# A two-block transformer kernel: where the inverse-root multiplication runs, and five orders on VectorE and ScalarE

## The reference

```python
def rmsnorm(x, g):
    y = xf * lax.rsqrt(jnp.mean(xf * xf, axis=-1, keepdims=True) + EPS)
    return (y * g)

def swiglu(x, w_gate, w_up, w_down):            # D_FF = 2816
    return (jax.nn.silu(x @ w_gate) * (x @ w_up)) @ w_down

# first block
x = x + 0.5 * swiglu(rmsnorm(x, ff1_norm), ff1_w_gate, ff1_w_up, ff1_w_down)
h = rmsnorm(x, mix_norm); a_in, q, k, v, g_logits = split(h @ w_in)
y_a = gmlp_spatial_gating(gelu(a_in), ln_g, ln_b, w_s, b_s)   # layernorm(v) inside
y_b = stick_breaking_attention(q, k, v)
merged = g_a * (y_a @ w_branch_a) + g_b * (y_b @ w_branch_b)
x = x + merged @ w_out
x = x + 0.5 * swiglu(rmsnorm(x, ff2_norm), ff2_w_gate, ff2_w_up, ff2_w_down)
x = rmsnorm(x, final_norm)
# second block: h + attention @ w_o, h + squared_relu_mlp, twice, and a last rms_norm
```

## Time and profile before

| what | us |
|---|---|
| median of 3 runs (1243.75 to 1244.47) | 1244.16 |
| the profiled execution | 1244.19 |
| its span | 1242.4 |
| TensorE busy in the span | 1224.5 (99%) |
| VectorE busy | 816.7 (66%) |
| ScalarE busy | 625.8 (50%) |
| GpSimd busy | 171.1 (14%) |

### The profile page before, as it was taken

One profiled execution on the slowest core, in us unless ns is written; L12 is line 12 of the kernel. 1 busy time (PEld: TensorE's weight loads), 2 busy tenths in 40 slices (PEclk: granted clock), 3 DMA queues, 4 the chain that ended last, 5 costly groups with the idle time before them and its releaser, 6 DMA issues.

```text
span 1242.4 us, 17592 instructions
## 1 busy us (share of the span) xinstructions
PE 1224.5 (99%) x6847; PEld 1047.5 (84%) x6847; DVE 816.7 (66%) x1229; ACT 625.8 (50%) x965; POOL 171.1 (14%) x224
## 2 busy tenths in 40 slices
PE   8999999999999999999999999999999999999997
PEld 7888888888878888888878988888888888888886
DVE  6766666344676667766676766875765576876764
ACT  6544436554644347444446566544446365744443
POOL 1222210122030003222102310000000541000000
PEclk9999999999999999999999999999999999999999
DMA  7755566533847455655665435865562555675540
GB/s 248 246 180 184 189 201 186 185 105 94 295 132 224 146 170 174 201 192 188 195 195 153 137 119 186 268 189 189 186 200 76 171 164 163 195 252 189 191 147 35
DMA packets 174907, 221.74 MB, mean 178 GB/s; under 512 B 9084, under 2 KB 103896, under 8 KB 174824
## 3 DMA queue, kind: packets, MB, share of 16 engines
q1 hardware_dynamic: 173496, 216.86, 55.2%
q0 software_dynamic: 880, 2.70, 0.8%
q10 hardware_dynamic: 448, 1.05, 0.2%
HBM read 219.52 MB, written 1.06 MB: 178 GB/s over the span
## 4 chain that ended last, share of the span: by engine, by line
PE 88%; DVE 6%; ACT 4%; issue 1%; DMA 0%; POOL 0%; ACTq 0%; DVEq 0%; POOLq 0%
PE bank L1431 48%; PE bank L1517 22%; PE bank L1524 11%; DVE w_lo L961 3%; PE bank L1454 1%; PE bank L1688 1%; ACT w_hi L618 1%; PE bank L1671 1%; PE bank L1661 1%; DVE xt L996 1%; ACT xt L656 1%; DVE x L1073 1%; DVE a_uv L1317 1%; PE bank L1648 1%; PE bank L1646 1%
## 5 line engine op out<-in xcount | busy, mean ns | idle before, releaser
L961 DVE TENSOR_TENSOR w_lo<-raw,w_hi 128x1024 fp32r<-128x1024 f32 (+1 forms) x448 | 499.2, 1137 | 234.3 <-ACT w_hi L618 234.0
L618 ACT ACTIVATE w_hi<-raw 128x1024 fp32r<-128x1024 f32 (+1 forms) x448 | 420.5, 972 | 278.3 <-PE bank L1524 146.6
L1517 PE MATMUL bank<-xt,w_hi 128*128 128x512 f32 x1216 | 316.6, 392 | 0.4 <-ACT w_hi L618 0.4
L1517 PEld LDWEIGHTS bank<-xt,w_hi 128*128 128x128 f32 x1216 | 215.8, 189 | 35.1 <-ACT w_hi L618 0.6
L1524 PEld LDWEIGHTS bank<-xt,w_lo 128*128 128x128 f32 x1216 | 170.6, 190 | 15.3
L1524 PE MATMUL bank<-xt,w_lo 128*128 128x256 f32 x1216 | 175.1, 282 | 0.0
L1431 PE MATMUL bank<-w_hi,xt 128*128 128x512 f32 x512 | 160.1, 394 | 1.9 <-DVE w_lo L961 1.1
L1431 PE MATMUL bank<-w_hi,yt_lo 128*128 128x512 f32 x336 | 132.2, 394 | 0.0
L1431 PE MATMUL bank<-w_hi,yt_hi 128*128 128x512 f32 x336 | 130.9, 390 | 0.0
L1431 PE MATMUL bank<-w_lo,yt_hi 128*128 128x512 f32 x336 | 130.9, 390 | 0.0
L1431 PE MATMUL bank<-xt,w_hi 128*128 128x256 f32 x640 | 115.9, 283 | 0.0
(11 more groups left out here) (198 smaller groups left out, 1202.1 us busy)
## 6 DMA issues: line engine op xcount, KB each, us to landing
raw<-in_w_up SPq DMA_DIRECT2D x64, 512.0 KB, 4.2
raw<-in_w_down SPq DMA_DIRECT2D x64, 512.0 KB, 4.4
raw<-in_w_in SPq DMA_DIRECT2D x56, 512.0 KB, 4.5
raw<-in_ff_w_gate SPq DMA_DIRECT2D x88, 256.0 KB, 2.9
raw<-in_ff_w_up SPq DMA_DIRECT2D x88, 256.0 KB, 3.2
raw<-in_ff_w_down SPq DMA_DIRECT2D x88, 256.0 KB, 4.4
raw<-in_moba_w_qkv SPq DMA_DIRECT2D x24, 512.0 KB, 4.2
raw<-in_w_o SPq DMA_DIRECT2D x16, 512.0 KB, 3.6
```

The lines of the kernel that those rows point to most:

```text
L618: act.activation(w_hi[:, c % RING, 0:w], raw[:, c % RAW, 0:w], ACT.Copy).then_inc(s["hi_ready"], 1)
L961: dve.tensor_tensor(w_lo[:, c % RING, 0:w], raw[:, c % RAW, 0:w], w_hi[:, c % RING, 0:w].bitcast(F32), ALU.subtract).then_inc(s["lo_ready" ...
L1517: ins = pe.matmul(up_banks(m)[q][:], w_h[:, k % 2, q * P:(q + 1) * P], flat(xt[:, k, :, :]), start=k == 0, stop=False, skip_group_check=True)
```

## The change

1. The multiplication by `rbc` in the gated feed-forwards is VectorE's in all eleven chunks; `normalized` is gone from GpSimd. VectorE waits for `rbc` once, in the first chunk. 40 instructions move.
2. In `ffn_end` VectorE prepares two units of the next phase before the first `add_half`, not four; the third comes behind it, the fourth behind the second `add_half`. This holds for ff1, ff2 and the first MLP.
3. In the first attention's cycle `second_part` of the next pair comes first on VectorE, ahead of `lo(c + 2)` and the copy of q.
4. The layer norm is sixteen VectorE instructions with two tensor inputs each (subtract the mean and multiply by the gain row, then multiply by the inverse deviation and add the bias row); GpSimd does none of it. VectorE waits for the rows.
5. At the start, turning x and preparing units alternate on ScalarE and VectorE, two column groups to one unit.
6. The row of gains of ff1 is sent by GpSimd's queue, ahead of its own first instructions, no longer by ScalarE's queue ahead of x.

```diff
@@ -452,6 +452,7 @@
                 count["n"] += 1
                 pool.wait_ge(s[name], count["n"])
 
+            pool.dma_start(gain_rows[0:8, :], ff1_norm.rearrange("a (k p) -> (a k) p", p=P)).then_inc(s["gain_in"], 16)
             pool.memset(eps[:], EPS).then_inc(s["zero_done"], 1)
             const(pool.memset(ident[:], 0.0))
             const(pool.affine_select(out=ident[:], in_=ident[:], compare_op=ALU.not_equal, fill=1.0, base=0,
...
@@ -545,28 +546,7 @@
                 if phase == "stick":
                     weights(PAIRS - 1)
 
-            def normalized(phase, n):
-
-                pool.wait_ge(s["rbc_done"], at(phase, "rbc_done") + 1)
-                by_token = rbc[:].unsqueeze(1).broadcast_to([P, 2, S])
-                for m in range(n - 1):
-                    for part in range(2):
-                        pool.wait_ge(s["g_done"], at(phase, "g_done") + 4 * m + 2 * part + 2)
-                        pool.tensor_tensor(work[1][:, part, :].rearrange("p (a b) -> p a b", a=2),
-                                           work[0][:, part, :].rearrange("p (a b) -> p a b", a=2), by_token,
-                                           ALU.mult).then_inc(s["nrm_done"], 1)
-
-            normalized("ff1", N_FF)
             pairs("stick")
-
-
-            pool.wait_ge(s["blk1_in"], 32)
-            for tok in range(TOK):
-                v = a_uv[:, tok, 0:D]
-                pool.wait_ge(s["ln_done2"], GROUPS * (tok + 1))
-                pool.tensor_tensor(v, v, ln_rows[0], ALU.mult).then_inc(s["lng_done"], 1)
-                pool.wait_ge(s["lng_done"], tok + 1)
-                pool.tensor_tensor(v, v, ln_rows[1], ALU.add).then_inc(s["v_ln"], 1)
 
 
             pool.wait_ge(s["x_done"], at("turn_ff2", "x_done"))
...
@@ -585,7 +565,6 @@
             pool.dma_start(wf[:], tiles(w_f_2)).then_inc(s["wf_in"], 16)
             pool.dma_start(bf[:], b_f_2.rearrange("(n a) -> n a", a=1)).then_inc(s["wf_in"], 16)
 
-            normalized("ff2", N_FF)
             pool.wait_ge(s["x_done"], at("stat_moba", "x_done"))
             pool.dma_start(row_gain[:], final_norm_2.rearrange("(a n) -> a n", a=1).broadcast_to([P, D]))\
                 .then_inc(s["row2_in"], 16)
...
@@ -602,8 +581,6 @@
         @block.scalar
         def _(act):
 
-            act.dma_start(gain_rows[0:8, :], ff1_norm.rearrange("a (k p) -> (a k) p", p=P))\
-                .then_inc(s["gain_in"], 16)
             act.dma_start(x[:, 1, :], x_in[0, P:2 * P, :]).then_inc(s["x_in"], 16)
             act.preload_act_table_set("sqrt_and_others")
...
@@ -644,10 +621,10 @@
                 act.wait_ge(s["rms_done"], at(phase, "rms_done") + 1)
                 act.activation(dst[:], rms[:], ACT.Exp, scale=-0.5).then_inc(s["rstd_done"], 1)
 
-            def turned(phase, half, sets):
+            def turned(phase, half, sets, parts=(0, 1)):
 
                 banks = turn_banks(phase, half)
-                for b in range(2):
+                for b in parts:
                     act.wait_ge(s["tr_ready"], at(phase, "tr_ready") + 2 * half + b + 1)
                     for k in range(4 * half + 2 * b, 4 * half + 2 * b + 2):
                         for dst, g in sets:
...
@@ -868,10 +845,8 @@
                     hi(b + u)
 
             act.wait_ge(s["gain_cols"], 1)
-            turned("turn_ff1", 0, [(xt_hi, 0)])
-            hi(0)
-            turned("turn_ff1", 1, [(xt_hi, 0)])
-            for u in range(1, AHEAD):
+            for u in range(AHEAD):
+                turned("turn_ff1", u // 2, [(xt_hi, 0)], (u % 2,))
                 hi(u)
             act.wait_ge(s["zero_done"], 1)
             ffn("ff1", N_FF, lambda: stat("stat_ff1", lambda: act.wait_ge(s["x_in"], 32)))
...
@@ -1014,7 +989,10 @@
                         dve.tensor_reduce(work[0][:, q // 2, (q % 2) * S:(q % 2 + 1) * S],
                                           up_banks(m)[q][:].rearrange("p (a b) -> p b a", a=2), AX_X, ALU.add)\
                             .then_inc(s["g_done"], 1)
-                        if gated and m == n - 1 and q % 2:
+                        if gated and q % 2:
+                            if m == 0 and q == 1:
+
+                                dve.wait_ge(s["rbc_done"], at(phase, "rbc_done") + 1)
 
                             dve.wait_ge(s["g_done"], at(phase, "g_done") + 4 * m + q + 1)
                             dve.tensor_tensor(work[1][:, q // 2, :].rearrange("p (a b) -> p a b", a=2),
...
@@ -1042,7 +1020,7 @@
                         dve.tensor_tensor(low, work[2][:, 1, :] if gated else work[1][:, t, :],
                                           high.bitcast(F32), ALU.subtract)\
                             .then_inc(s["ht_lo"], 1)
-                    for u in range(10 if m < n - 1 else 8, 12):
+                    for u in (10, 11) if m < n - 1 else (8, 9):
                         lo(c + u)
 
                 ahead()
...
@@ -1076,8 +1054,10 @@
             def ffn_end(phase, scale, between):
                 b = at(phase, "units") + dict(PHASES)[phase]["units"]
                 add_half(phase, scale, 0, b - 3)
+                lo(b + 2)
                 between()
                 add_half(phase, scale, 1, b - 1)
+                lo(b + 3)
 
             def attention(phase, kind, turn_b, stats):
                 b = at(phase, "units")
...
@@ -1132,16 +1112,12 @@
                 def cycle(c, pr, e):
 
                     first_part(pr + 1)
-                    if kind == "stick":
-                        lo(c + 2)
-                        q_evac(c, e)
-                    elif pr:
+                    if kind != "stick" and pr:
                         y_part(pr - 1)
                     second_part(pr + 1)
-                    if kind != "stick":
-                        q_evac(c, e)
-                        lo(c + 2)
-                    elif pr:
+                    q_evac(c, e)
+                    lo(c + 2)
+                    if kind == "stick" and pr:
                         y_part(pr - 1)
                     k_evac(c, e)
                     lo(c + 3)
...
@@ -1271,10 +1247,8 @@
             dve.wait_ge(s["gain_ready"], 1)
             dve.tensor_copy(gain[:, 0:8], bank[2][:, 0:8]).then_inc(s["gain_cols"], 1)
             dve.wait_ge(s["gain_cols"], 1)
-            turned("turn_ff1", 0, [(xt_lo, xt_hi, 0)])
-            lo(0)
-            turned("turn_ff1", 1, [(xt_lo, xt_hi, 0)])
-            for u in range(1, AHEAD):
+            for u in range(AHEAD):
+                turned("turn_ff1", u // 2, [(xt_lo, xt_hi, 0)], (u % 2,))
                 lo(u)
 
             def first_stats():
...
@@ -1311,11 +1285,20 @@
             dve.wait_ge(s["lns_done"], 1)
             dve.reciprocal(ln_rstd[:], ln_rstd[:]).then_inc(s["lnr_done"], 1)
             dve.wait_ge(s["lnr_done"], 1)
+            dve.wait_ge(s["blk1_in"], 32)
             for n in range(TOK * GROUPS):
                 tok, g = divmod(n, GROUPS)
-                v = a_uv[:, tok, g * GD:(g + 1) * GD]
-                dve.tensor_scalar(v, v, bn2[:, n, 0:1], ln_rstd[:, n:n + 1], ALU.subtract, ALU.mult)\
-                    .then_inc(s["ln_done2"], 1)
+                cols = slice(g * GD, (g + 1) * GD)
+                v = a_uv[:, tok, cols]
+                dve.scalar_tensor_tensor(v, v, bn2[:, n, 0:1], ln_rows[0][:, cols], ALU.subtract, ALU.mult)\
+                    .then_inc(s["lng_done"], 1)
+            for n in range(TOK * GROUPS):
+                tok, g = divmod(n, GROUPS)
+                cols = slice(g * GD, (g + 1) * GD)
+                v = a_uv[:, tok, cols]
+                dve.wait_ge(s["lng_done"], n + 1)
+                dve.scalar_tensor_tensor(v, v, ln_rstd[:, n:n + 1], ln_rows[1][:, cols], ALU.mult, ALU.add)\
+                    .then_inc(s["v_ln"], 1)
             dve.wait_ge(s["gate_in"], 64)
             chunks("gates", gate_bias)
...
@@ -1873,7 +1856,7 @@
             pe.wait_ge(s["y_lo"], PAIRS)
             for n in range(TOK * GROUPS):
                 tok, g = divmod(n, GROUPS)
-                pe.wait_ge(s["v_ln"], tok + 1)
+                pe.wait_ge(s["v_ln"], GROUPS * (tok + 1))
                 ins = pe.matmul(bank[4 + 2 * tok + g // 2][:, (g % 2) * GD:(g % 2 + 1) * GD], wst[:, g, :],
                                 a_uv[:, tok, g * GD:(g + 1) * GD], start=True, stop=True)
                 if g % 2:
```

2 lines of the change are left out of this document (1 added, 1 removed).

## The result

The changed kernel takes 1236.9 us (median of 6 runs, 1236.17 to 1237.62), the kernel before 1244.85 beside it (6 runs, 1243.75 to 1245.7). The ratio is 0.9936, 95% interval 0.9923 to 0.9949, so it is faster by 7.95 us. The forecast was 1236.3, in the range 1235.0 to 1239.6. The total was nearly right; one of its terms, the start, was wrong in sign.

The account below looks back on a forecast made before the run. TensorE bounds the kernel, busy 1224.5 of 1242.4 us, so only its losses between instructions can be won back. The terms 0.6 + 2.6 - 0.1 + 3.0 + 1.8 = 7.9 us off 1244.19 gave 1236.3, range 1235.0 to 1239.6.

Parts of the forecast that it names:

- Edit 1, nothing: Gated feed-forward chunks: VectorE's added 1.4 us costs nothing, with 9.5 us of slack to down products, 3 for reductions.
- Edit 2, 2.6 (2.0 to 2.7): Ends of both gated feed-forwards: additions to x come earlier, saving 1.3 us each; the MLP's end costs 0.1.
- Edit 3, 3.0 (2.0 to 3.1): First attention: VectorE's second part put first removes six TensorE waits, 2.0 us idle plus 6 x 0.16 of overlap.
- Each hides 0.16 us of overlap, of which about 0.1 is taken by the switch to this form also without a wait: First attention's six waits: each costs 0.16 us beyond its idle time; the 0.1 switch offsets a first pair 0.70, not 0.60.
- Edit 4, 1.8 (1.3 to 1.9): Layer norm: sixteen VectorE instructions in 6.4 us with GpSimd silent let preparations keep up, returning 1.8 us to TensorE.
- The start, 0.6 less (0 to 1.0): Kernel start: second half of x, sent at 0.80, lands about 0.6 us earlier and is turned from 6.1 to 6.2.
- A small transfer of GpSimd's lands 3.3 us after issue, at 4.1: Start: the gain row on GpSimd's queue lands at 4.1 us, before TensorE asks for it at about 4.6.
- The gain row comes late on GpSimd's queue: Start, rival: row lands at 5.3 us, x turned 0.9 later, alternation returns 0.4; time 1237.4; chance 0.08.
- the identity was to delay TensorE's transposes to 2.28: Start: GpSimd issues the gain row before making the identity, so transposes begin at 2.28, not 1.69; ready for x at 6.1.
- a new releaser with over 1 us in TensorE's waits: Sign that the prediction is wrong: TensorE waits over 1 us in total for something it did not wait for before.
- a first product later than 10.58: Sign that the prediction is wrong, at the start: TensorE's first product comes after 10.58 us.
- x's first transpose at 6.1 to 6.2: Sign that the prediction is right, at the start: TensorE begins turning x at 6.1 to 6.2 us.

Follow-up runs that it names:

- e1: The changed kernel with the gain row sent first on ScalarE's queue again, ahead of the second half of x: 1235.57 us, ratio 0.9927 to the kernel before.
- e6: The kernel before with only the gain row's transfer moved from ScalarE's to GpSimd's queue: 1245.99 us, ratio 1.0013.

## Why the prediction was right, and where not

**Edit 1, nothing.** Right. Slack of 9.6 and 2.7 us in a chunk as told. The price of VectorE's pair is 0.692 each, all 44 of them. What the prediction didn't see is that chunk 1 has no such cover, since its weights land late: there 0.69 us of VectorE can be TensorE's. Started early, e1 lost 0.48 us; the changed kernel, late from its start, nothing.

**Edit 2, 2.6 (2.0 to 2.7).** Right: 2.69, and 2.69 alone. The MLP's end cost 0.0 and not the 0.1 of the sum.

**Edit 3, 3.0 (2.0 to 3.1).** Mechanism right, size too small: 3.64, alone 3.61. The failed step is "Each hides 0.16 us of overlap, of which about 0.1 is taken by the switch to this form also without a wait". The cycle went from 9.82 us (242.62 to 252.44) to 9.35 (241.04 to 250.39), so one wait of 0.21 idle had cost 0.47 and not 0.37. The prediction set the switch's 0.1 against the longer first pair of products (0.70 us behind a wait, 0.60 without), and so left both out. But the switch takes nothing: the first product of the new form starts 0.12 us after the last of the old one (240.92 to 241.04), which is the step of those. The 0.1 of the pair stays, six times, and 2.0 + 6 x 0.26 = 3.6.

**Edit 4, 1.8 (1.3 to 1.9).** Right: 1.72. Sixteen instructions took 6.34 us, 6.4 by the neighbour of the earlier trace rows. The estimate that rested on the Trainium skill, page VectorE: DVE Perf Modes (section The TRN2 errata), 6.8 us and a wait of 0.4, was too long. One record is 0.480 us here (3.26 less 7 steps of 0.397), more than its 0.424, but the instructions follow each other 0.397 apart. The remaining wait was 0.2.

**The start, 0.6 less (0 to 1.0).** Wrong: 0.94 more, give or take the clock. The step that failed is "A small transfer of GpSimd's lands 3.3 us after issue, at 4.1". It was issued at 1.32, not 0.80, and took 5.1 us, not 3.3, with one megabyte of x and the first weights in flight. The earlier trace rows is of a transfer with other work around it. x itself was early, as foretold: its last packet ended at 5.44 us and not, as in e1, at 6.14. The rival "The gain row comes late on GpSimd's queue" is what came: it said landing at 5.3, x turned 0.9 later, 0.4 given back, 1237.4. Measured: 6.4, 1.03, 0.57 and 1236.9. e1 and e6 show it from both sides (-1.3 and +1.6 us). The rival had been given a chance of 0.08, too little for an operation of which the trace had only a distant relative. A second step failed beside it: the identity was to delay TensorE's transposes to 2.28, and they began at 2.92. By the prediction's own sum TensorE is then ready for x at 6.74 - 1.22 + 1.23 = 6.75, so nothing of the 0.6 was to be had in this order even with a row in time (an estimate). And the sum had no term for the clock.

Two of the prediction's own signs of being wrong came true, both at the start: a new releaser with over 1 us in TensorE's waits (the row, 1.2) and a first product later than 10.58 (11.04). Of what it expected to see, only x's first transpose at 6.1 to 6.2 did not come.

So the total held in part by luck. Attention and ends gave 0.8 more than forecast, the layer norm 0.1 and the start 1.5 less. That leaves 7.1 of 7.9 us up to the last matmul, and 7.4 in the profiled time (1244.19 to 1236.78). The medians' 7.95 comes so near to 7.9 because the kernel before ran 0.7 us longer beside the changed one (1244.85) than on record before (1244.16).
